# Norm sums and roots taken per token on the partitions, and two modulation chunks moved, in a two-layer hybrid block on one Trainium2 core

## The reference

```python
def rms_norm(x, g):
    xf = x.astype(jnp.float32)
    y = xf * lax.rsqrt(jnp.mean(xf * xf, axis=-1, keepdims=True) + EPS)
    return (y * g.astype(jnp.float32)).astype(x.dtype)
...
    cond = jax.nn.silu(c)
    for l in range(DEPTH):
        mod = cond @ ada_w[l] + ada_b[l]
        sh1, sc1, g1, sh2, sc2, g2 = jnp.split(mod, 6, axis=-1)
        h = modulate(rms_norm(x, mix_norm_g[l]), sh1, sc1)
        mix = token_mixer(h, w_in[l], conv_w[l], conv_b[l], dt_bias[l], a_log[l], d_skip[l],
                          ssd_norm_g[l], pool_w[l], pool_scale[l], w_out[l])
        x = x + g1[:, None, :] * mix
        h = modulate(rms_norm(x, ffn_norm_g[l]), sh2, sc2)
        x = x + g2[:, None, :] * peer_ffn(h, peer_wq[l], peer_keys[l], peer_u[l], peer_v[l])
    return rms_norm(x, final_norm_g)
```

## Time and profile before

| | |
|---|---|
| median of 3 runs | 3059.4 us (3054.8 to 3063.73) |
| the profiled execution | 3056.11 us, its span 3054.3 us |
| busy share of the span | PE 97%, PEld 90%, DVE 83%, ACT 48%, POOL 31% |
| chain that ended last | PE 84%, DVE 6%, DMA 5%, ACT 2% |

### The profile page before, as it was taken

How to read it: one execution, slowest core, us unless ns; L and a number is a source line. 1 busy time by engine, 2 the same in 40 slices (tenths; PEclk the granted TensorE clock), 3 DMA queues, 4 the chain that set the end, 5 groups by cost and what they waited for, 6 DMA issues and landing times.

```text
span 3054.3 us, 48434 instructions
## 1 busy us (share of the span) xinstructions
PE 2965.3 (97%) x17464; PEld 2756.2 (90%) x17464; DVE 2548.0 (83%) x4940; ACT 1470.7 (48%) x2352; POOL 945.0 (31%) x709
## 2 busy tenths in 40 slices
PE   6999999999999999999989989999999999999998
PEld 4766789999999999999977668999999999999997
DVE  4666789898997799889886769998888868899888
ACT  4343234488885333333353532445888733333333
POOL 1000026644443333333300000565444443333331
PEclk9999999999999999999999999999999999999999
DMA  7424646699999999999932112568999899999996
GB/s 271 172 90 166 248 143 197 233 327 385 355 347 344 359 357 354 363 356 352 359 100 69 50 62 84 162 194 318 343 372 376 305 376 347 362 357 356 358 365 221
DMA packets 252361, 836.75 MB, mean 274 GB/s; under 512 B 24640, under 2 KB 57664, under 8 KB 241472
## 3 DMA queue, kind: packets, MB, share of 16 engines
q1 hardware_dynamic: 158336, 453.50, 41.8%
q0 software_dynamic: 89280, 348.17, 31.0%
q10 hardware_dynamic: 4608, 33.56, 2.6%
HBM read 751.24 MB, written 83.89 MB: 273 GB/s over the span
## 4 chain that ended last, share of the span: by engine, by line
PE 84%; DVE 6%; DMA 5%; ACT 2%; issue 1%; POOL 0%; SPq 0%; DVEq 0%; ACTq 0%; POOLq 0%
PE bank L962 37%; PE bank L1450 31%; PE bank L1418 5%; PE bank L1260 3%; DMA w_raw<-wst 3%; PE bank L978 2%; DMA ring<-u,gidx 1%; PE bank L1018 1%; DVE w_lo L1492 1%; ACT w_hi L680 1%; PE bank L1340 1%; DMA pj<-adaw 1%; PE bank L1236 1%; PE bank L1247 1%; PE bank L1432 0%
## 5 line engine op out<-in xcount | busy, mean ns | idle before, releaser
L680 ACT ACTIVATE w_hi<-w_raw 128x1024 fp32r<-128x1024 f32 x596 | 630.5, 1058 | 837.2 <-PE bank L962 650.7
L1492 DVE TENSOR_TENSOR w_lo<-w_raw,w_hi 128x1024 fp32r<-128x1024 f32 x522 | 639.1, 1224 | 345.4 <-ACT w_hi L680 343.5
L962 PE MATMUL bank<-hH,w_hi 128*128 128x368 f32 (+1 forms) x2528 | 882.7, 349 | 13.9 <-ACT w_hi L680 8.3
L962 PE MATMUL bank<-hH,w_lo 128*128 128x368 f32 (+1 forms) x2528 | 862.0, 341 | 0.0
L962 PE MATMUL bank<-hL,w_hi 128*128 128x368 f32 (+1 forms) x2528 | 861.3, 341 | 0.0
L1450 PE MATMUL bank<-c_hi,w_hi 128*128 128x368 f32 x2048 | 676.1, 330 | 2.6 <-DVE w_lo L1492 2.4
L1450 PE MATMUL bank<-c_lo,w_hi 128*128 128x368 f32 x2048 | 674.3, 329 | 0.0
L1450 PE MATMUL bank<-c_hi,w_lo 128*128 128x368 f32 x2048 | 673.1, 329 | 0.0
L644 POOL DMA_INDIRECT ring<-u,gidx x288 | 409.5, 1422 | 468.0 <-DVE gact L1977 431.7
L644 POOL DMA_INDIRECT ring<-v,gidx x288 | 331.9, 1153 | 691.9 <-DVE vacc L1989 630.7
L962 PEld LDWEIGHTS bank<-hH,w_hi 128*128 128x128 f32 x2528 | 476.0, 188 | 60.1 <-issue 23.5
(11 more groups left out here) (314 smaller groups left out, 2987.7 us busy)
## 6 DMA issues: line engine op xcount, KB each, us to landing
w_raw<-wst SPq DMA_DIRECT2D x596, 512.0 KB, 6.1
activations<-act_out SPq DMA_DIRECT2D x128, 368.0 KB, 7.2
act_in<-activations SPq DMA_DIRECT2D x64, 736.0 KB, 7.3
gate_matrices<-stage ACTq DMA_DIRECT2D x32, 1024.0 KB, 9.9
gates<-gate_matrices SPq DMA_DIRECT2D x64, 512.0 KB, 9.7
ada_buf<-adaw POOLq DMA_DIRECT2D x24, 1024.0 KB, 7.3
nrm<-adaw POOLq DMA_DIRECT2D x8, 1024.0 KB, 5.1
pj<-adaw POOLq DMA_DIRECT2D x7, 1024.0 KB, 7.0
```

Source lines behind the costliest of these rows:

```text
L680: nc.scalar.activation(w_hi[g % 2][:, :, :].rearrange("p a b -> p (a b)"), w_raw[:, g % RAWS, :], ACT.Copy).then_inc(s_wh, 1)
L962: last = mm(bank[s][:, 0:t.stop - t.start], a[s][:, k, :], b[:, k, t], start=(k == 0 and a is w_hi and b is hH), stop=(k == KT - 1 and a i ...
L1492: v.tensor_tensor(w_lo[g % 2][:, :, :].rearrange("p a b -> p (a b)"), w_raw[:, g % RAWS, :], w_hi[g % 2][:, :, :].rearrange("p a b -> p (a ...
```

## The change

A sum per token is now made with the squares as the stationary matrix and one column of ones as the moving one, so it comes out as a column: token on the partition, four columns for 512 tokens. The root is taken on 128x4 elements (128x8 for y) and brought back to rows over all partitions by products of the column, broadcast to 128x128, with the identity; the scaling reads these rows from PSUM. Tiles 0 to 3 of a norm of x still go through the group sums, tiles 4 to 7 are added one by one. `GAP_ADA` is 3.

```diff
-GAP_ADA = 5
+GAP_ADA = ADA_SLOTS
...
-    return [GAP_ADA + 2 * n, GAP_ADA + 2 * n + 1] if n < 4 else [n + 9]
+    return [GAP_ADA + 2 * n, GAP_ADA + 2 * n + 1] if n < 6 else [n + 9]
...
-            def seed_root(psum, eps, dst, sem_out):
-
-                steps.link(nc.scalar.activation(nrm[:, 0, :], psum, ACT.Ln, bias=eps))
-                nc.scalar.activation(dst, nrm[:, 0, :], ACT.Exp, scale=-0.5).then_inc(sem_out, 1)
+            def seed_root(psum, c, eps, sem_out):
+
+                steps.link(nc.scalar.activation(nrm[:, 0, c], psum, ACT.Ln, bias=eps))
+                nc.scalar.activation(nrm[:, 2, c], nrm[:, 0, c], ACT.Exp, scale=-0.5).then_inc(sem_out, 1)
...
+                act.wait_ge(s_yss, l + 1)
+                seed_root(bank[1][:, 0:2 * NT], slice(2 * NT, 4 * NT), eps_y, s_yroot)
                 att_weights(0)
-                for g in range(2):
-                    act.wait_ge(s_yss, l * 2 + g + 1)
...
-            def norm_total(m):
-
-                pe.wait_ge(s_part, m + 1)
-                mm(bank[3][:, :], ones[:, :], nrm[:, 1, :], start=True, stop=True).then_inc(s_ssum, 1)
+            def token_sums(src, first=False, last=False):
+
+                if first:
+                    mm(bank[3][:, 0:NT], ident[P // 2:P, :], ident[P // 2:P, 0:NT], start=True, stop=False)
+                for tb in range(NT):
+                    ins = mm(bank[3][:, tb:tb + 1], src[:, tb * P:(tb + 1) * P], ones[:, 0:1],
+                             start=False, stop=last and tb == NT - 1)
+                if last:
+                    ins.then_inc(s_ssum, 1)
+
+            def norm_sums(m, ks):
+
+                for k in ks:
+                    if k == 6:
+                        pe.wait_ge(s_part, m + 1)
+                        token_sums(nrm[:, 1, :])
+                    pe.wait_ge(s_sq, m * KT + k + 1)
+                    token_sums(h32[:, k, :], first=(k == 4), last=(k == KT - 1))
+
+            def norm_rows(m):
+
+                pe.wait_ge(s_nroot, m + 1)
+                for tb in range(NT):
+                    ins = mm(bank[2][:, tb * P:(tb + 1) * P], nrm[:, 2, tb:tb + 1].broadcast_to([P, P]), ident[:, :],
+                             start=True, stop=True)
+                ins.then_inc(s_rows, 1)
...
                 for g in range(2):
-                    for k in range(2):
-                        last = mm(bank[g][:, :], ones[:, :], y_tok[:, 2 * g + k, :], start=(k == 0), stop=(k == 1))
-                    last.then_inc(s_yss, 1)
+                    for tb in range(NT):
+                        for k in range(2):
+                            last = mm(bank[1][:, g * NT + tb:g * NT + tb + 1], y_tok[:, 2 * g + k, tb * P:(tb + 1) * P],
+                                      ones[:, 0:1], start=(k == 0), stop=(k == 1))
+                last.then_inc(s_yss, 1)
...
-                att_sums(1)
+                att_sums(1, range(0, 1))
+                pe.wait_ge(s_ynroot, l + 1)
+                for g in range(2):
+                    for tb in range(NT):
+                        c = (2 + g) * NT + tb
+                        last = mm(bank[g][:, tb * P:(tb + 1) * P], nrm[:, 2, c:c + 1].broadcast_to([P, P]), ident[:, :],
+                                  start=True, stop=True)
+                    last.then_inc(s_yrows, 1)
+                att_sums(1, range(1, NT))
...
-                norm_groups(2 * l + 1, 0)
-                norm_groups(2 * l + 1, 4)
-                norm_total(2 * l + 1)
+                norm_groups(2 * l + 1)
+                norm_sums(2 * l + 1, (4, 5, 6, 7))
                 if l == 0:
-                    for c in range(GAP_ADA):
+                    ada_chunk(1, 0)
+                norm_rows(2 * l + 1)
+                if l == 0:
+                    for c in range(1, GAP_ADA):
                         ada_chunk(1, c)
...
                 att_arg(0)
+                y_root()
                 mixed_low(1, 4, 6)
```

More of the change, by code:

```diff
@@ L227, in ada_place @@
         def ada_place(n):
[L229 to L232, removed]
             if n < 3 or n >= ADA_CHUNKS:
@@ L399, in build @@
         s_root = sem("root_ready")
+        s_nroot = sem("newton_root_ready")
+        s_rows = sem("root_rows_done")
         s_x = sem("x_updated")
@@ L442, in build @@
         s_yroot = sem("y_root_ready")
+        s_ynroot = sem("y_newton_root_ready")
+        s_yrows = sem("y_root_rows_done")
         s_pool = sem("pooled_ready")
@@ L498, in ada_sem @@
                 return s_ada0[n], 16
-            in_gap = lambda m: ADA_SLOTS <= m - ADA_CHUNKS < GAP_ADA
-            if in_gap(n):
-                return s_gap[n - ADA_CHUNKS - ADA_SLOTS], 16
             s = n % ADA_SLOTS
-            return s_ada[s], 16 * len([m for m in range(s, n + 1, ADA_SLOTS) if m >= KT and not in_gap(m)])
+            return s_ada[s], 16 * len([m for m in range(s, n + 1, ADA_SLOTS) if m >= KT])
         block = ctx.enter_context(nc.Block())
@@ L982, in project_pair, with norm_groups @@
                             last.then_inc(s_tile, 1)
-            def norm_groups(m, k0):
-                pe.wait_ge(s_sq, m * KT + k0 + 4)
+            def norm_groups(m):
+                pe.wait_ge(s_sq, m * KT + 4)
                 for j in range(4):
[L988 to L991, removed]
-            def norm_total(m):
-                pe.wait_ge(s_part, m + 1)
-                mm(bank[3][:, :], ones[:, :], nrm[:, 1, :], start=True, stop=True).then_inc(s_ssum, 1)
+                    last = mm(bank[2][32 * j:32 * j + 32, :], ones[:, 0:32], h32[:, j, :], start=True, stop=True)
+                last.then_inc(s_gsum, 1)
+            def token_sums(src, first=False, last=False):
[19 more added lines that the diff above has]
+                ins.then_inc(s_rows, 1)
             pe.sem_inc(s_taken, 2)
@@ L1043, in _ @@
                         ada_chunk(0, c)
+                norm_rows(2 * l)
+                if l == 0:
                     modulation(0, 0, 4)
@@ L1226, in att_scores, with att_sums @@
                     last.then_inc(s_z, 1)
-                def att_sums(h):
+                def att_sums(h, rows=range(NT)):
                     pe.wait_ge(s_nlk, l * 4 + h + 1)
@@ L1232, in att_sums @@
                         pe.wait_ge(s_zv, l * SCORES + h + 2)
-                    for i in range(NT):
+                    for i in rows:
                         b, o = ATT_BANK[h % 2][i]
@@ L1237, in att_sums @@
                                       nlk[h % 2][:, O4[j]:O4[j] + W4[j]], start=(j == i), stop=(j == NT - 1))
-                    last.then_inc(s_cum, 1)
+                    if rows[-1] == NT - 1:
+                        last.then_inc(s_cum, 1)
                 def att_out(h):
```

45 lines of the change are left out of this document (23 added, 22 removed).

## The result

The changed kernel takes 3074.49 us (median of 5 runs, 3070.43 to 3083.05) against 3057.87 us for the kernel before (5 runs, 3054.15 to 3063.73). The ratio is 1.0057, 95% interval 1.0035 to 1.0079: it is slower, by 16.6 us between the medians. The prediction said 3056.3 us, range 3047 to 3069, with a sum of -3.1. Its first rival, "one-column products don't hold PE's clock", said 3071.5.

A forecast was written before the change was run, and what follows sets the result against it. PE was taken as the bound (84% of the chain), with each norm serial over PE, ACT and DVE. Terms 0.3 + 0.3 + 0.5 - 0.2 - 4.4 - 1.4 + 1.8 = -3.1 us gave 3056.3 us, range 3047 to 3069.

The forecast's parts named there:

- first rival: One-column sums in norms and y: PE's clock falls to 1.2 GHz, +15 on the forecast, 3071.5 us; chance 0.2.
- Prices of the new pieces: Costs of new operations: 0.23 us per one-column product, 0.26 per product bringing roots back, scaling from PSUM nothing extra.
- granted clock 1.00 through the one-column products: Sign to check in the changed kernel's timeline: PE's clock stays full during the per-token sums.
- norm 4: Last norm, at the end: PE is the queue, group and small products, then shorter root and rows; -0.2 us.
- four small ACT and DVE prices: Root steps on small tiles: about 0.20 us per DVE step on 128x4, about 0.25 per ACT step.
- norm 0: First norm: sums fill PE's wait for the last chunk and rows its second wait; +0.3 us, up to +1.3.
- norm 1: Savings on ACT and DVE and an earlier copy are eaten by eleven further loads and the rows; +0.3 us.
- norms 2 and 3: Same PE and ACT list as the norm before them: +0.3 and +0.2, together +0.5 us.
- y, both, with the clock at `att_out(1)`: Norm of y, twice: `att_arg(1)` comes earlier, -4.4 us; less slow clock at `att_out(1)`, -1.4 us.
- second rival: Shorter waits around the norms and in y keep the clock up: 11.5 us lower, 3045; chance 0.2.
- The chunks: Query projection tiles 4 and 5 get a second chunk, 0.9 us each, +1.8; in the gap they cost nothing.
- Against: Argument against the first rival: PE had waited before the slow modulation, and eight four-column products ran at full speed.

The follow-up runs named there:

- wide64: The changed kernel with each per-token sum moving 64 equal columns of ones instead of one; 3060.0 us, ratio 1.0016 to the kernel before.
- after_again: The changed kernel as it is, run once more for a second trace; one run, 3068.6 us.
- bursts: The kernel before with 4 to 48 extra products ahead of every second query projection tile; 32 took 10.0 us with one column, 7.1 with 64.
- groups1: The changed kernel with all eight tiles of a norm of x in the group sums, then four one-column products; 3056.3 us, ratio 0.9998.
- groups64: As groups1, with 64 columns instead of one in the four products of a norm of x and sixteen of y; 3054.9 us, ratio 0.9986.
- y1only: The kernel before with only the change's norm of y, its sixteen sums with one column; 3054.9 us, ratio 0.9997.

## Why the prediction was wrong

**The step that failed is "Prices of the new pieces".** It priced the one-column product at 0.23 from rows at full clock, and the sum took the clock of 1.00 for granted; "granted clock 1.00 through the one-column products" was the check. It failed in norms 0 to 3 and in y of layer 0, and in norm 4 in the second trace; in the first the fall comes right behind the sums there. The sum has no term for it, only a rival at 0.2. With the clock held, as wide64 shows it, the seven stretches give -1.6; in the two traces of the changed kernel they gave +15.0 and +9.1. The size of a product was right (1.95 for eight, 0.24), also the four small ACT and DVE prices (0.21 to 0.27, 0.16) and the scaling from PSUM (1.41 for two operations, before 1.42).

| | forecast | after | after_again | wide64 |
|---|---|---|---|---|
| norm 0 | +0.3 | +6.4 | +4.6 | +2.1 |
| norm 1 | +0.3 | +4.0 | +1.5 | +0.5 |
| norms 2 and 3 | +0.5 | +4.6 | +3.6 | +2.0 |
| norm 4 | -0.2 | +1.1 | +3.0 | +0.8 |
| y, both, with the clock at `att_out(1)` | -5.8 | -1.1 | -3.6 | -7.0 |
| sum | -4.9 | +15.0 | +9.1 | -1.6 |

The last column is the nearest to the prediction's own kernel, one in which the clock holds through the sums; its opening product takes 0.3 more a norm than that of 4 columns, and 0.7 more in norm 0. Norm 1 is +0.5 for +0.3, y -7.0 for -5.8. The chain was read nearly rightly and the clock was not.

**The first rival's working** gave +2.5 for each of norms 1 to 4 on top of +0.6, so 10.6; measured 9.7 and 8.1. That is the sum alone: one by one they were 4.0, 1.5, 3.1 and 1.1, so that it comes so near is in part luck. For y it left -0.8 each; measured 0.0 and -1.1, then -1.2 and -2.4. Only norm 0 was far off: it added 1 for slow rows, but the clock stays low over the chunks that come next, three at 1.93 instead of 1.04 to 1.06, the fourth at 1.30.

**Norm 0** was also mis-sized without a fall in the sums: +2.1 in wide64, of which 0.7 is wide64's own opening product (1.14 from 23.27 on, for 0.39 with 4 columns). There the last chunk starts at 32.75, 2.1 later than the 30.62 of the earlier trace rows, where I had let the sums pass the transfer's wait by 0.7. The sums and the zero product took 5.9 and not 4.8 (from 23.27 to 26.34 and from 27.33 to 30.15), and what fell away was 1.4 and not 1.9; 5.9 - 1.4 - 2.19 is 2.3. And the two excesses that the prediction had, 0.7 and 0.3, were not added but only the last one taken. **Norm 4** has a slip of its own: it priced the 21 small products at 4.6, where 21 x 0.23 is 4.8; from 3044.60 to 3049.91 they take 5.3 in wide64, 4.9 in the changed kernel.

**Norm 2** is 12.1 in after and in wide64 alike: the clock falls there ahead of the pair in every trace, as it did before the change, and now the rows stand in the slow stretch too (2.08 in wide64, 1.16 in its norm 1). The second rival, shorter waits keep the clock up, had hoped for the contrary and is wrong: with 64 columns the waits are in pieces of 1.26 ahead of the rows and 2.47 behind them, and the pair still starts slow (0.63 a record at 1565.70, for 0.39).

**y** without a fall is what the prediction said, as wide64 shows in layer 0:

```profile
202.11 3.76 PE L1319 MATMUL bank<-ones,y_tok 128*128 128x64 f32 x32
...
212.09 1.68 DVE L1832 TENSOR_TENSOR pj<-zs,bank 128x512 f32<-128x512 f32 x4 [0.35 <-PE bank L1253]
...
220.72 2.37 PE L1265 MATMUL bank<-pj,v_tok 128*64 128x512 f32 x8 [1.68 <-DVE pj L1845]
```

The sums start at 202.11, `att_arg(1)` at 212.09, 10.0 behind (forecast 10.0, before 12.4), idle until PE's sums; `att_out(1)` at 220.72, 18.6 behind (forecast 18.9, before 21.1). There it ran at full clock, so the whole 2.2 came, of which a third was taken, and that is why the term was too small. In the changed kernel the fall within the sums pushed `att_arg(1)` back to 13.3; that one column is its cause in y is not shown, since it comes with 64 columns too.

**The chunks** cost 0.9 each in tiles 4 and 5 as forecast: 8.46 from one close of a tile to the next (350.52 and 358.98), before 7.56. In the changed kernel's gap the cover is gone: one chunk stands ahead of the rows and two behind them, and PE goes from the last one to the pair without an idle time.

**The range** ended at 3069 and the median is 3074.5. The rival had its mechanism, its place and nearly its size; what was wrong was its chance. Its "Against", that "eight such products at 198.38 ran at full speed", was no evidence: bursts of 4 and 8 passed, 12 did not, and the norms have 20.

What stays open: why some traces have two falls more between norm 2 and y of layer 1 (groups1, groups64, y1only, burst and one of the two of wide64), which moves a single trace by 4 us; what drops the clock in y of layer 0; and whether wide64, level with before by its stretches (-1.6 + 1.8), is truly 3 us slower (ratio 1.0016, from 1.0004 on).

## What to carry to other kernels

A stretch of products that move only a few columns is not cheap filler: PE's row says busy, and the clock may halve for this stretch and for the dense work behind it. Bring the tiles together with a full-width product first, so that few such products are left, or let them move 64 equal columns, which cost next to nothing (2.00 us for eight, 1.95 with one) and took the loss of this kernel from 16.6 to 3.1 us. Neither is a guarantee: the clock also fell behind four one-column products in norm 1 of groups1, and with 64 columns in y of layer 0 in two traces of five. In a profile, compare the mean of one form at two places before you trust a busy share, and price a new form not only by its duration but by a stretch as long as the one planned.

## What the runs showed that was not expected

- 32 products of 64 or 128 columns were faster than 32 of one or sixteen: 7.1 us against 10.0 and 10.7, since the first kept a granted clock of 1.00 and the second did not. A float32 product's two passes cost about 0.12 us each up to 128 columns (eight products in 1.95 at one column, 1.96 at 16, 2.00 at 64 and 2.05 at 128).
- PE's clock fell with PE busy for 100% of the stretch and no idle time ahead of it. The Trainium skill, TensorE: Matmul & The Clock Gate, section HAM oscillation, has waits as the cause; the bursts show a fall without any. Its section PE-mode transpose says of transposes that they don't count as busy; no run here timed one, but the one-column products behave so in the bursts of 12 and more.
- Twelve one-column products were enough (2.8 us), and the fall then came 0.5 us behind them, in the next products of 512 columns, which went from 0.39 to 0.63 us.
